# Two-block transformer on one core: the router's products with its weights stationary and both token tiles moving, its scores turned back by TensorE

## The chip, the cores and the metric

The kernel runs on one core of a Trainium2 chip. The metric is the time of one execution on the device in microseconds (us), the median of several runs. Engines are named as in the profile: PE is TensorE (PEld its loading of stationary operands), DVE VectorE, ACT ScalarE, POOL GpSimd, SP SyncE, which issues the loads.

## The reference

256 tokens of 1024 features pass a first block of two layers (gated feed-forward, a hybrid attention, gated feed-forward) and a second block of two layers. A layer of the second block is a mixer with a layer norm, and then this, on which the change works:

```python
ple = (p[i] @ ple_w_proj[i]) * jax.nn.sigmoid(x @ ple_w_gate[i])
ffn = grouped_moe(x, router_w, router_bias, moe_w1[i], moe_w3[i], moe_w2[i])
x = layer_norm_2(DEEPNORM_ALPHA * x + ffn + ple, ln_ffn_g[i], ln_ffn_b[i])

def grouped_moe(x, router_w, router_bias, w1, w3, w2):   # 16 experts in 4 groups, 2 chosen of one group
    scores = jax.nn.sigmoid((xt @ router_w).astype(F32))          # 256 x 16
    sel = scores + router_bias.astype(F32)
    grp_score = jnp.sum(lax.top_k(grp, TOP_K)[0], axis=-1)
    ...
    gates = jnp.sum(jax.nn.one_hot(idx, N_EXPERTS, dtype=F32) * w[..., None], axis=1)
    h = jax.nn.silu(jnp.einsum('td,edf->etf', xt, w1)) * jnp.einsum('td,edf->etf', xt, w3)
    h = h * gates.T[:, :, None].astype(h.dtype)
    y = jnp.einsum('etf,efd->td', h, w2)
```

## The kernel before

Tokens are two tiles of 128 (t = 0 and 1). The token rows `x` are turned by TensorE into `xt_hi` and `xt_lo`, a high part in a reduced format and the rest of it, each 128 x 8 x 256: features on the partitions, tokens along the row. Weights come in units of 1 MB on SyncE's queue into a ring of six buffers, and each is split the same way, the high part by ScalarE (line 1413), the low part by VectorE (line 1869). A product is three matmuls (`mm3`, lines 627 to 631; in the trace L629, L630, L631): high by high, high by low, low by high. `four` (line 649) does four blocks of 128 features, that is twelve matmuls, of one unit for one token tile: the tokens are stationary and 512 columns of weights move. `four` can call something ahead of its last block, `meanwhile`.

`before_experts` is written once for each engine and runs in both layers of the second block. On TensorE (line 1160) it does, in this order: `route(0)`, the router's product for tile 0, 24 matmuls with 128x128 tokens stationary and the router's 16 columns moving; `four` with the first unit for tile 0; the turn of tile 1 (`turn_x(1)`, eight transposes, which wait for VectorE's layer norm of that tile, line 1970); `four` with the second unit for tile 0; `route(1)`; `four` with both units for tile 1, each followed by a release of its unit (`unit_used`); one more unit for both tiles; a wait for `gates_ready`; five small products that number the chosen tokens (line 1188); the last unit; the turn of the small input `p`; the gather of the first experts' tokens (line 1154); the projection of `p`.

On ScalarE (line 1742) `scores(t)` takes the sigmoid of the 16 scores of a tile's 128 tokens (line 1745) into `r_s`, with splits of weights between the two. On VectorE (line 2415) come the low part of tile 1, two splits, and then the routing decisions: lines 2425 to 2462, some forty small operations one behind the other, up to `gates_ready`.

The experts (`gathered_experts`) run in eight pairs. Six buffers of 2 MB hold a pair's weights. `load_experts` (line 361) gives the order of the loads: the buffer of the first load is free when the stage begins, the next two wait for the first unit released in `before_experts`, two more for the third, one for the fourth, and the first two loads of the second pair for the end of the stage (`unit_used`); every later load waits until TensorE has used its buffer (`moe_used`). All of them stand in SyncE's one queue.

Of the kernel before, what the change touches and what calls it, by code (L numbers as in the profile page):

```python
# [19 lines left out]
ALU = mybir.AluOpType  # L20
# [6 lines left out]
P = 128  # L27
T = 256
TT = T // P
# [97 lines left out]
def program(nc, a, out):  # L127
    with ExitStack() as ctx:
# [6 lines left out]
        def sem(name):  # L135
            return ctx.enter_context(nc.semaphore(name))
# [133 lines left out]
        routed = sem("routed")  # L270
        route_sig = sem("route_sig")
# [121 lines left out]
        def carve(tensor, at, *dims):  # L393
            n = int(np.prod(dims))
            v = tensor[:, at:at + n]
            if len(dims) == 1:
                return v
            names = "abcd"[:len(dims)]
            return v.rearrange(f"p ({' '.join(names)}) -> p {' '.join(names)}",
                               **{k: d for k, d in zip(names[1:], dims[1:])})  # L400
# [72 lines left out]
        ple_gate = carve(work, 0, TT, D)  # L473
        r_s = carve(work, 13600, TT, N_EXPERTS)
# [160 lines left out]
        def _(pe):  # L635
# [524 lines left out]
            def before_experts(l):  # L1160
                def route(t):
                    pe.wait_ge(xt_lo_ready, seen(xt_lo_ready, 2))
                    for k in range(KD):
                        mm = mm3(pe, h_bank[t][:, 0:N_EXPERTS], xt_part(k, t), (rw_hi[:, k, :], rw_lo[:, k, :]),
                                 k == 0, k == KD - 1)
                    mm.then_inc(routed, 1)

                pe.wait_ge(rw_lo_ready, 1)
                route(0)
                w = []  # L1170
                for u in range(2):
                    w.append(unit(4))
                    four(y_bank[0][0][:, :], w[u], u, 0)
                    if u == 0:
                        turn_x(1)
                route(1)
                for u in range(2):
                    four(y_bank[1][0][:, :], w[u], u, 1).then_inc(unit_used, 1)
# [220 lines left out]
        def _(act):  # L1399
# [342 lines left out]
            def before_experts(l):  # L1742
                def scores(t):
                    act.wait_ge(routed, seen(routed))
                    act.activation(r_s[:, t], h_bank[t][:, 0:N_EXPERTS], ACT.Sigmoid).then_inc(route_sig, 1)

                scores(0)
                high_xt(1)
                split_to(4)
                scores(1)  # L1750
# [104 lines left out]
        def _(dve):  # L1855
# [559 lines left out]
            def before_experts(l):  # L2415
# [7 lines left out]
                dve.wait_ge(route_sig, seen(route_sig, TT))  # L2423
                bias = router_b.rearrange("p (o e) -> p o e", o=1).broadcast_to([P, TT, N_EXPERTS])
                link(dve.tensor_tensor(r_sel, r_s, bias, ALU.add))
# [303 lines left out]
```

## Time and profile before

| | us |
|---|---|
| median of 3 runs | 1782.88 (1781.55 to 1783.09) |
| profiled execution | 1785.93 |
| its span, first to last instruction | 1784.2 |
| TensorE busy | 1714.1 (96%) |
| VectorE busy | 925.7 (52%) |
| ScalarE busy | 630.7 (35%) |
| mean granted clock of TensorE | 0.986 |

Times of the trace are microseconds from the start of the span. A row of a timeline gives start, duration, engine, line, operation, what is written and read, the shape (stationary rows * columns, then partitions x moving columns) and how many instructions were merged; in brackets stand the idle time of the engine before it and what ended it. Matmuls are pipelined: the duration of one is longer than the distance of two starts, and the distance is the pace. The granted clock is 1.00 at 2.4 GHz and 0.50 at 1.2 GHz.

### The profile page before, as it was taken

The page shows a single profiled execution, that of the slowest core. Times are in us where ns is not written, and L with a number is a line of the kernel's source. Part 1 is how long each engine was busy: PE and PEld are TensorE (multiplying, and loading weights), DVE is VectorE, ACT ScalarE, POOL GpSimd, SP SyncE. Part 2 cuts the span into 40 slices and gives each one's busy share as a digit, 9 for nine tenths or more (in the row PEclk, how much of TensorE's full clock was granted, in tenths as well). Part 3 has the DMA queues.
Part 4 walks back from the last instruction along what each step waited for, and adds up shares of the span by engine and source line. Part 5 has one row for each costly group of instructions (what it writes and reads, how often), then busy time and mean ns, then how long its engine had stood idle before and what let it go on. Part 6 is the DMA issues. An engine that isn't in the chain of part 4 may idle for free.

```text
span 1784.2 us, 21897 instructions
## 1 busy us (share of the span) xinstructions
PE 1714.1 (96%) x8828; PEld 1244.3 (70%) x8828; DVE 925.7 (52%) x1342; ACT 630.7 (35%) x826; POOL 108.8 (6%) x89
## 2 busy tenths in 40 slices
PE   7999999999999999999899998999997999999996
PEld 6888777778878887777787787644443877744442
DVE  4754757674555546676685587511114566511113
ACT  4544443454425444443544364111112354111110
POOL 1000060000000000602000000000000000000000
PEclk9999999999999999999999999999998999999998
DMA  7555540655555555406454434899997533899994
GB/s 297 189 188 188 190 164 7 232 186 188 188 189 188 188 188 192 182 6 233 162 188 165 152 140 167 354 409 428 428 428 312 195 118 129 346 415 426 430 425 209
DMA packets 46803, 419.79 MB, mean 235 GB/s; under 512 B 5280, under 2 KB 5280, under 8 KB 8832
## 3 DMA queue, kind: packets, MB, share of 16 engines
q1 hardware_dynamic: 43200, 405.82, 58.2%
q0 software_dynamic: 3520, 12.78, 2.1%
q8 instruction: 62, 1.02, 0.2%
q14 instruction: 21, 0.17, 0.0%
HBM read 417.53 MB, written 1.05 MB: 235 GB/s over the span
## 4 chain that ended last, share of the span: by engine, by line
PE 83%; DVE 7%; DMA 4%; ACT 3%; POOL 1%; issue 1%; DVEq 0%; SPq 0%; POOLq 0%; ACTq 0%
PE hh L1237 11%; PE y L629 10%; PE y L631 10%; PE y L630 10%; PE hh L629 8%; PE hh L631 8%; PE hh L630 8%; DMA wide<-pairs 3%; PE turn L1154 3%; PE hh L1269 3%; PE turn L1269 3%; DVE w_lo L1869 2%; ACT w_hi L1413 1%; PE y L1281 1%; DMA raw<-units 1%; PE turn L747 1%
## 5 line engine op out<-in xcount | busy, mean ns | idle before, releaser
L1869 DVE TENSOR_TENSOR w_lo<-raw,w_hi 128x2048 fp32r<-128x2048 f32 x181 | 411.2, 2290 | 154.3 <-ACT w_hi L1413 153.5
L1413 ACT ACTIVATE w_hi<-raw 128x2048 fp32r<-128x2048 f32 x193 | 365.3, 1912 | 70.3 <-DMA raw<-units 66.1
L629 PE MATMUL hh<-w_hi,xt_hi 128*128 128x512 f32 x704 | 280.5, 398 | 8.0 <-DVE w_lo L1869 4.8
L631 PE MATMUL hh<-w_hi,xt_lo 128*128 128x512 f32 x704 | 276.0, 392 | 0.0
L630 PE MATMUL hh<-w_lo,xt_hi 128*128 128x512 f32 x704 | 275.5, 391 | 0.0
L1237 PE MATMUL hh<-wide,work 128*64 128x512 f32 x880 | 197.7, 599 | 4.8 <-DMA wide<-pairs 4.8
L629 PE MATMUL y<-w_hi,xt_hi 128*128 128x512 f32 (+1 forms) x464 | 184.8, 398 | 6.1 <-DVE xt_lo L2410 3.1
L630 PE MATMUL y<-w_lo,xt_hi 128*128 128x512 f32 (+1 forms) x464 | 180.5, 389 | 0.0
L631 PE MATMUL y<-w_hi,xt_lo 128*128 128x512 f32 (+1 forms) x464 | 180.4, 389 | 0.0
L629 PEld LDWEIGHTS hh<-w_hi,xt_hi 128*128 128x128 f32 x704 | 133.1, 189 | 36.6 <-DVE w_lo L1869 5.2
L631 PEld LDWEIGHTS hh<-w_hi,xt_lo 128*128 128x128 f32 x704 | 132.9, 189 | 28.6
L629 PE MATMUL y<-w_hi,ht_hi 128*128 128x512 f32 x368 | 145.7, 396 | 6.9 <-DVE w_lo L1869 6.7
L630 PEld LDWEIGHTS hh<-w_lo,xt_hi 128*128 128x128 f32 x704 | 133.3, 189 | 26.5
L1237 PEld LDWEIGHTS hh<-wide,work 128*64 128x64 f32 x880 | 61.9, 138 | 126.5 <-issue 117.4
L631 PE MATMUL y<-w_hi,ht_lo 128*128 128x512 f32 x368 | 144.2, 392 | 0.0
L630 PE MATMUL y<-w_lo,ht_hi 128*128 128x512 f32 x368 | 144.0, 391 | 0.0
L1431 ACT ACTIVATE gate_h<-hh 128x256 f32<-128x256 f32 x88 | 33.4, 383 | 214.0 <-PE hh L631 213.8
L629 PEld LDWEIGHTS y<-w_hi,xt_hi 128*128 128x128 f32 x464 | 89.0, 192 | 26.5 <-DVE xt_lo L1976 3.6
L569 POOL TENSOR_TENSOR rstd<-moments,minus_half 128x1 f32<-128x1 f32 x20 | 21.4, 1070 | 1345.1 <-DVE moments L1962 1345.1
L631 PEld LDWEIGHTS y<-w_hi,xt_lo 128*128 128x128 f32 x464 | 89.1, 192 | 18.1
L630 PEld LDWEIGHTS y<-w_lo,xt_hi 128*128 128x128 f32 x464 | 89.2, 192 | 16.3
L629 PEld LDWEIGHTS y<-w_hi,ht_hi 128*128 128x128 f32 x368 | 69.5, 189 | 24.2 <-DVE w_lo L1869 8.0
(344 smaller groups left out, 1957.8 us busy)
## 6 DMA issues: line engine op xcount, KB each, us to landing
raw<-units SPq DMA_DIRECT2D x193, 1024.0 KB
wide<-pairs SPq DMA_DIRECT2D x85, 2048.0 KB
late<-pairs SPq DMA_DIRECT2D x7, 1024.0 KB
raw<-pairs SPq DMA_DIRECT2D x7, 1024.0 KB
spare<-pairs SPq DMA_DIRECT2D x2, 2048.0 KB
xt_wide<-pairs SPq DMA_DIRECT2D x2, 2048.0 KB
ln_gb<-ln_g POOLq DMA_DIRECT2D x6, 512.0 KB, 3.9
ln_gb<-ln_b POOLq DMA_DIRECT2D x6, 512.0 KB, 5.5
```

What stands on the lines that cost most here:

```text
L569: pool.tensor_tensor(rstd[:, t], moments[:, t, 1:2], minus_half[:, 0:1], ALU.pow).then_inc(rstd_ready, 1)
L629: pe.matmul(dst, left[0], right[0], start=start, stop=False)
L630: pe.matmul(dst, left[0], right[1], start=False, stop=False)
L631: return pe.matmul(dst, left[1], right[0], start=False, stop=stop)
L747: mm = pe.transpose(turn_bank[0][:, k * T + t * P:k * T + (t + 1) * P], h[:, t, k * P:(k + 1) * P], ident[:, :])
L1154: mm = pe.matmul(dst[:, k * P:(k + 1) * P], x[:, t, at * P:(at + 1) * P], pick[:, p, t, :], start=t == 0, stop=t == TT - 1)
L1237: mm = pe.matmul(dst[half(b), :], xe[:, p, 4 * u + k, half(b)], w[b][:, k, :], start=u == 0 and k == 0, stop=u == 1 and k == 3)
L1269: mm = pe.matmul(dst[half(b), :], turned[:, k, half(b)], w[b][:, k, :], start=k == 0, stop=k == 3)
L1281: mm = pe.matmul(y_bank[t][c][:, :], spread[:, p, t * P:(t + 1) * P], part[:, c, :], start=first and part is ye_hi, stop=last and part is ...
L1413: act.activation(hi[r][:, :], raw[r][:, :], ACT.Copy).then_inc(hi_ready, 1)
L1431: act.activation(gate_act[:, t], h_bank[t][:, 0:HALF], ACT.Silu).then_inc(gate_ready, 1)
L1869: dve.tensor_tensor(lo[r][:, :], raw[r][:, :], hi[r][:, :].bitcast(F32), ALU.subtract)\
```

## The change

The router's weights become the stationary operand, 128 x 16, and the high or low part of both token tiles moves, 256 columns. So one set of 24 matmuls gives all scores, as 16 rows of 256 tokens, in `h_bank[0]`. It stands where `route(1)` stood; `route(0)` is gone. ScalarE takes one sigmoid of 16 x 256 into `score_t`, a new name for a part of `work`. TensorE turns it back with two transposes (`turn_scores`) into `h_bank[1]`, 128 tokens by 16 scores for each tile; it does so within the first `four` for tile 1, ahead of its last three matmuls, behind a wait for the sigmoid. VectorE waits for these transposes (`route_turned`) instead of the sigmoids, adds the bias from PSUM, and copies the scores to `r_s`.

```diff
--- before.py
+++ after.py
@@ -268,6 +268,7 @@
         rw_hi_ready = sem("rw_hi_ready")
         rw_lo_ready = sem("rw_lo_ready")
         routed = sem("routed")
+        route_turned = sem("route_turned")
         route_sig = sem("route_sig")
         gates_ready = sem("gates_ready")
         p_loaded = sem("p_loaded")
@@ -471,6 +472,7 @@
 
 
         ple_gate = carve(work, 0, TT, D)
+        score_t = work[0:N_EXPERTS, 13824:13824 + T]
         r_s = carve(work, 13600, TT, N_EXPERTS)
         r_sel = carve(work, 13632, TT, N_EXPERTS)
         r_two = carve(work, 13664, 8, TT * N_GROUPS)
@@ -1158,24 +1160,31 @@
                 mm.then_inc(gathered[l], 1)
 
             def before_experts(l):
-                def route(t):
-                    pe.wait_ge(xt_lo_ready, seen(xt_lo_ready, 2))
+                def route():
                     for k in range(KD):
-                        mm = mm3(pe, h_bank[t][:, 0:N_EXPERTS], xt_part(k, t), (rw_hi[:, k, :], rw_lo[:, k, :]),
-                                 k == 0, k == KD - 1)
+                        mm = mm3(pe, h_bank[0][0:N_EXPERTS, 0:T], (rw_hi[:, k, :], rw_lo[:, k, :]),
+                                 (xt_hi[:, k, :], xt_lo[:, k, :]), k == 0, k == KD - 1)
                     mm.then_inc(routed, 1)
 
-                pe.wait_ge(rw_lo_ready, 1)
-                route(0)
+                def turn_scores():
+                    pe.wait_ge(route_sig, l + 1)
+                    for t in range(TT):
+                        mm = pe.transpose(h_bank[1][:, t * N_EXPERTS:(t + 1) * N_EXPERTS], score_t[:, t * P:(t + 1) * P],
+                                          ident[0:N_EXPERTS, 0:N_EXPERTS])
+                    mm.then_inc(route_turned, 1)
+
                 w = []
+                pe.wait_ge(xt_lo_ready, seen(xt_lo_ready, 2))
                 for u in range(2):
                     w.append(unit(4))
                     four(y_bank[0][0][:, :], w[u], u, 0)
                     if u == 0:
                         turn_x(1)
-                route(1)
+                pe.wait_ge(rw_lo_ready, 1)
+                pe.wait_ge(xt_lo_ready, seen(xt_lo_ready, 2))
+                route()
                 for u in range(2):
-                    four(y_bank[1][0][:, :], w[u], u, 1).then_inc(unit_used, 1)
+                    four(y_bank[1][0][:, :], w[u], u, 1, meanwhile=turn_scores if u == 0 else None).then_inc(unit_used, 1)
                 last = unit(4)
                 for t in range(TT):
                     mm = four(y_bank[t][1][:, :], last, 0, t)
@@ -1740,14 +1749,10 @@
                 stage_done(S5_UNITS)
 
             def before_experts(l):
-                def scores(t):
-                    act.wait_ge(routed, seen(routed))
-                    act.activation(r_s[:, t], h_bank[t][:, 0:N_EXPERTS], ACT.Sigmoid).then_inc(route_sig, 1)
-
-                scores(0)
                 high_xt(1)
                 split_to(4)
-                scores(1)
+                act.wait_ge(routed, l + 1)
+                act.activation(score_t, h_bank[0][0:N_EXPERTS, 0:T], ACT.Sigmoid).then_inc(route_sig, 1)
                 split_to(PLE_UNITS)
                 for j in range(2):
                     wait_units(2 * j + 2)
@@ -2420,9 +2425,12 @@
                 dve.tensor_copy(tri.rearrange("p a c -> p (a c)"), tri_ones).then_inc(dve_link, 1)
                 dve.wait_ge(dve_link, seen(dve_link))
 
-                dve.wait_ge(route_sig, seen(route_sig, TT))
+                dve.wait_ge(route_turned, l + 1)
                 bias = router_b.rearrange("p (o e) -> p o e", o=1).broadcast_to([P, TT, N_EXPERTS])
-                link(dve.tensor_tensor(r_sel, r_s, bias, ALU.add))
+                turned_s = h_bank[1][:, 0:TT * N_EXPERTS].rearrange("p (t e) -> p t e", t=TT)
+                dve.tensor_tensor(r_sel, turned_s, bias, ALU.add).then_inc(dve_link, 1)
+                dve.tensor_copy(r_s, turned_s).then_inc(dve_link, 1)
+                dve.wait_ge(dve_link, seen(dve_link, 2))
                 four = r_sel.rearrange("p t (g e) -> p (t g) e", g=N_GROUPS)
                 for i, (u, v, op) in enumerate(((0, 1, ALU.max), (0, 1, ALU.min), (2, 3, ALU.max), (2, 3, ALU.min))):
                     dve.tensor_tensor(r_two[:, i], four[:, :, u], four[:, :, v], op).then_inc(dve_link, 1)
```

## Rows read from the trace of the kernel before

**Rows 1.** The page, part 4: the chain that ended last, by engine.

```profile
PE 83%; DVE 7%; DMA 4%; ACT 3%; POOL 1%; issue 1%; DVEq 0%; SPq 0%; POOLq 0%; ACTq 0%
```

**Rows 2.** Timeline of TensorE, layer 0 before the experts.

```profile
1105.47 0.17 PE L629 MATMUL hh<-rw_hi,xt_hi 128*128 128x16 f32 x1
...
1108.07 0.49 PE L629 MATMUL y<-w_hi,xt_hi 128*128 128x512 f32 x1
...
1111.73 0.48 PE L629 MATMUL y<-w_hi,xt_hi 128*128 128x512 f32 x1
...
1114.55 0.17 PE L629 MATMUL hh<-rw_hi,xt_hi 128*128 128x16 f32 x1
...
1117.93 0.61 PE L629 MATMUL y<-w_hi,xt_hi 128*128 128x512 f32 x1
...
1121.33 0.41 PE L631 MATMUL y<-w_hi,xt_lo 128*128 128x512 f32 x1
...
1129.79 0.62 PE L1188 MATMUL hh<-slot_mem 128*128 128x16 f32 x5
```

**Rows 3.** Timeline of VectorE, the same stage.

```profile
1108.90 1.41 DVE L1970 SCALAR_TENSOR_TENSOR x_rows<-x_rows,rstd,ln_gb 128x512 f32<-128x512 f32 x2
...
1118.13 0.19 DVE L2425 TENSOR_TENSOR work<-work,params 128x32 f32<-128x32 f32 x1
...
1128.91 0.23 DVE L2462 TENSOR_SCALAR gates<-work 128x16 f32<-128x16 f32 x1
```

**Rows 4.** Timeline, VectorE's norm and TensorE's turn of the first tile.

```profile
1100.75 1.42 DVE L1970 SCALAR_TENSOR_TENSOR x_rows<-x_rows,rstd,ln_gb 128x512 f32<-128x512 f32 x2 [0.54 <-POOL rstd L569]
...
1101.56 1.32 PE L661 MATMUL turn<-ident,x_rows 128*128 128x128 f32 x8 [1.83 <-DVE x_rows L1970]
...
1102.63 0.48 PE L629 MATMUL y<-w_hi,xt_hi 128*128 128x512 f32 x1
```

**Rows 5.** Timeline of TensorE, products with 256 moving columns.

```profile
1078.06 0.28 PE L630 MATMUL hh<-xt_lo,w_hi 128*128 128x256 f32 x1
...
1083.56 0.28 PE L631 MATMUL hh<-xt_hi,w_lo 128*128 128x256 f32 x1
```

**Rows 6.** The page, its part 5: busy, mean ns of one; idle before.

```profile
L1431 ACT ACTIVATE gate_h<-hh 128x256 f32<-128x256 f32 x88 | 33.4, 383 | 214.0 <-PE hh L631 213.8
```

**Rows 7.** Timeline, two transposes and who reads them.

```profile
1315.07 0.44 PE L1249 MATMUL turn<-ident,work 128*128 128x128 f32 x2
...
1315.54 0.42 DVE L2542 TENSOR_SCALAR slot_mem<-turn 128x256 fp32r<-128x256 f32 x1 [5.25 <-PE turn L1249]
```

**Rows 8.** Timeline of VectorE and TensorE, layer 1.

```profile
1511.78 1.42 DVE L1970 SCALAR_TENSOR_TENSOR x_rows<-x_rows,rstd,ln_gb 128x512 f32<-128x512 f32 x2
...
1521.02 0.19 DVE L2425 TENSOR_TENSOR work<-work,params 128x32 f32<-128x32 f32 x1
...
1532.66 0.62 PE L1188 MATMUL hh<-slot_mem 128*128 128x16 f32 x5
```

**Rows 9.** SyncE's issues; stretches: length, engines' busy, clock, DMA share, GB/s.

```profile
1121.77 0.83 SPq L359 DMA_DIRECT2D wide<-pairs  x2
...
1145.63 0.83 SPq L359 DMA_DIRECT2D wide<-pairs  x2
...
1118.00:1119.00 1.00, 1.00 (x4) 0.81 (x3) 0.90 (x9) 1.00 (x1) 0.00 (x0) 0.50 0.00 0
1178.00:1179.00 1.00, 1.00 (x8) 0.29 (x6) 0.00 (x0) 0.34 (x1) 0.00 (x0) 1.00 0.65 262
```

**Rows 10.** Timeline of TensorE behind two idle times, and stretches behind them.

```profile
997.83 0.50 PE L629 MATMUL hh<-w_hi,xt_hi 128*128 128x512 f32 x1 [2.12 <-ACT work L1665]
...
1751.70 1.77 PE L1237 MATMUL hh<-wide,work 128*64 128x512 f32 x6 [2.25 <-DMA wide<-pairs]
...
999.00:1000.00 1.00, 1.00 (x3) 0.78 (x3) 0.62 (x1) 0.00 (x0) 0.00 (x0) 0.50 0.00 0
1753.00:1754.00 1.00, 1.00 (x4) 0.24 (x2) 0.00 (x0) 0.00 (x0) 0.00 (x0) 0.50 1.04 442
```

## The prediction

> **What bounds the kernel now.** I read the page first. TensorE carries 83% of the chain that ended last [rows 1], so a stage is worth what it delays on TensorE, unless a wait takes over. The profiled execution took 1785.93 us, 1784.2 of it span; the median of the three runs is 1782.88. The sum below is made in times of the profiled execution, and its difference is put on the median.
>
> Then the timeline of TensorE in layer 0's stage before the experts [rows 2]. Products of the router run twice: 24 matmuls of 16 columns from 1105.47 to 1108.07 (2.60 us) and 24 more from 1114.55 on, 0.11 us each. Between and behind them stand groups of 12 matmuls of 512 columns; the group from 1111.73 to 1114.55 takes 2.82 us. From 1121.33 to 1129.79 there are 37 in 8.46 us, 0.229 us each. No row of TensorE from 1105.47 to 1129.79 carries idle time.
>
> The timeline of VectorE [rows 3] shows the second line of work: the second tile's rows are normalised by 1108.90 + 1.41 = 1110.31; the routing decisions start at 1118.13 and their last step ends at 1128.91 + 0.23 = 1129.14. That start carries no idle time, so it follows VectorE's own splits and not the scores; by their pace the products end near 1117.2. TensorE comes to the products that need the gates at 1129.79, only 0.65 us after they are ready. That slack is the number on which this case turns: the change takes work from TensorE, but its gates come by VectorE.
>
> Last the loads [rows 9]. No bytes move at 1118, since the next expert weights wait for a freed unit; they are issued at 1121.77. Those of the second pair are issued at 1145.63, when TensorE has finished this stage. At 1178 the DMA engines drop to 262 GB/s: they have caught up with what TensorE releases. After such a point their position depends on TensorE's releases and not on when the stream began. So what counts per layer is when TensorE gets into the experts.
>
> **Part by part, layer 0.** The first 24 small matmuls go, and the 12 wide ones behind them start 2.60 us earlier, at 1105.47, and end near 1108.3. Then TensorE turns the second tile, which VectorE finishes at 1110.31 as before: nothing in its path changed. For the first tile the same hand-over is in the trace: normalised at 1100.75 + 1.42 = 1102.17, next wide matmul at 1102.63 [rows 4], 0.46 us. So the next 12 start at 1110.77 and not 1111.73: of 2.60 us only 0.96 is left, the rest turns into a wait for VectorE of about 1.4 us. Behind the waiting transposes are queued all matmuls of TensorE; ScalarE and VectorE wait for the turned tile and get it 0.9 us earlier.
>
> They end at 1110.77 + 2.82 = 1113.59. The high and low halves of the turned tile, for which the router waits, are in time: before, TensorE came to the second small products as long after the transposes as now, and without idle time.
>
> The new router is 24 matmuls with 16 columns stationary and 256 moving. No row has this form. From below its pace is 0.11 us (the old form), from above 0.229 us (512 columns). I take the row with 256 moving columns and 128 stationary: 46 steps from 1078.06 to 1083.56 [rows 5], 0.12 us. That makes 2.88 us (bounds 2.6 and 5.5), ending at 1116.47.
>
> The Trainium skill, TensorE: Matmul & The Clock Gate, section LDWEIGHTS, has a load take time by its stationary columns, so that 16 would cost next to nothing. Its section Back-to-back issue gap gives 262 cycles for 256 moving columns, which at 2.4 GHz is an estimate of 0.109 us: 2.62 us for 24 where the row makes it 2.88, and the sum 0.26 us less per layer. The same page's section on Fast Weight Load speaks against the change: only loads of 128 columns that aren't FP32 are fast. No run here shows a load of 16 columns.
>
> Nine wide matmuls follow, 2.82 - 3 x 0.229 = 2.13 us, to 1118.60. They cover ScalarE's sigmoid. Its row has 128x256 at 383 ns [rows 6]; with a hand-over of 0.1 us it is done near 1117.0, and 1.6 us of cover is left. Were that gone, TensorE would wait on it with all its queue. Two transposes of 16 columns each follow. The nearest rows are two of 128 columns: start at 1315.07, VectorE reads them at 1315.54 and TensorE is busy on them for 0.44 us [rows 7]. So 0.47 us until VectorE and 0.44 of TensorE (bounds 0.2 and 0.8). VectorE starts on the decisions at 1119.07, not at 1118.13: it has ended its splits 0.9 us earlier than before and now waits for this turn. The added copy of the scores costs a step, 0.09 us. The decisions take 1129.14 - 1118.13 = 11.01 us as before, and the hand-over to TensorE 0.10 (half of the normalising ended at 1100.75 + 0.71 = 1101.46, the transposes started at 1101.56 [rows 4]). TensorE gets the gates at 1130.27, against 1129.79: 0.48 us later.
>
> TensorE itself is there at 1118.60 + 0.44 + 39 x 0.229 = 1127.97. It saved 1.82 us and then waits 2.30 us for VectorE. Behind that wait are its next 24 matmuls, the turn of the small input, the gather for the first experts, and SyncE's loads that these release.
>
> The same sum in layer 1 [rows 8]: rows normalised at 1511.78 + 1.42 = 1513.20; 0.46 + 2.82 + 2.88 + 2.13 + 0.47 later VectorE starts, at 1521.96 (before: 1521.02); 0.09 + 11.01 + 0.10 make 1533.16 against 1532.66, 0.50 us later. Both layers: 0.98 us later.
>
> Expert loads: the unit that releases them is used up near 1118.60 + 0.44 + 2 x 0.229 + 0.4 = 1119.9 instead of 1121.33 + 0.41 = 1121.74 [rows 2], so they start 1.8 us earlier. I cost that gain at nothing. Four slots and the extra one are all that may be loaded before TensorE has ended the stage, and the next wait for its releases (the load at 1145.63, then the drop at 1178) is 0.48 us later than before. Were these points not binding, the earlier start would be worth up to 1.8 us a layer.
>
> **The clock.** Before, the second small products are followed by half clock, 1.2 GHz: from 1117.93 to 1121.33 eight wide matmuls take 3.40 us [rows 2], where 8 x 0.229 is 1.83, so 1.57 us are lost; the granted clock is 0.50 at 1118 [rows 9]. Much of that was harmless, since TensorE had slack to the gates. The change takes these products away, and the 1127.97 is worked out without that loss. But it makes a new quiet stretch: 2.30 us between starts, some 2.1 as the trace counts idle time, with the five small products behind it (0.47 us). In the trace, idle times of 2.12 us (at 997.83) and 2.25 us (at 1751.70) were followed by half clock, with 0.50 granted at 999 and at 1753 [rows 10]. An idle time of 1.83 us was not: the matmul behind the transposes there lasts 0.48 us, where one at half clock lasts 0.61 [rows 4, 2]. Of this layer's two stretches of small products only the second was. So I give each layer's wait somewhat under an even chance of a half-clock stretch, which then lies on TensorE's path in full: 1.57 us. One of the two layers hit is the likeliest: 0.98 + 1.57 = 2.55 us, a span of 1786.75 for the profiled 1784.2 and 1785.4 on the median.
>
> **Rivals.**
> 1. No layer is hit: 0.98 us later, 1783.9. For it speaks that 1.83 us of idle time kept the full clock.
> 2. Slower side: both layers are hit, 0.98 + 2 x 1.57 = 4.12 us, 1787.0. It decides where both waits for the gates are followed by half clock; for it speaks that both rows above 2 us lost the clock, against it that the first stretch of small products, 2.60 us long, did.
> 3. Faster side: VectorE isn't late, because the gates' slack is larger than I think, and TensorE's whole saving of 1.82 us a layer arrives: 3.64 us less, 1779.2. The 0.65 us of slack speak against it.
> 4. The change doesn't make the products cheap: 16 stationary columns count for little, and the new products (2.88 us) are followed by half clock like the old ones, in front of the turned scores. Then the decisions start up to 1.57 us later in a layer: 0.98 + 1.57 per layer hit, 1785.4 or 1787.0. Its upper bound of pace, 0.229 us, would cost 2.6 us a layer and give 1789.1.
>
> **How the numbers follow.** One stretch hit 0.42, none 0.32, both 0.14, the products as in rival 4 0.07, the whole saving or most of it 0.05. The predicted time is that of the first, 1785.4. The range takes in rivals 1 and 2 with the bounds of the small costs (the page's pace and the lower bound for the transposes take 0.5 us a layer off, to 1782.9, and a fraction of a microsecond of slack gained to about 1782): 1781.9 to 1787.3. Faster or slower by over 0.2% (3.57 us, about what a measurement of this kernel can tell from no change) is below 1779.3 or above 1786.45. Faster has only the full case of rival 3: 0.04. Slower has rival 2 and a part of rival 4: 0.16. The rest is 0.80.
>
> **What would show it.** No 16-column router matmuls; 24 of 256 columns at 0.12 us. Idle time of TensorE of 1.3 to 1.5 us before the turn of the second tile. VectorE idle before its first routing step, until the two transposes. TensorE idle for 2.1 us before the five small products, where it had none. First expert load behind the spare one 1.8 us earlier, the one at 1145.63 later. Half clock behind the gates' wait or not decides between the forecast and rivals 1 and 2. I am wrong at the root if TensorE doesn't wait for the gates, or if the end of the experts moves with the first loads instead of with TensorE's entry.

## The result, and the profile after

| | before | after |
|---|---|---|
| median, 13 runs each, us | 1782.2 (1778.33 to 1784.76) | 1784.99 (1783.6 to 1787.33) |
| ratio after / before, 95% interval | | 1.0016 (1.0009 to 1.0024) |
| profiled execution, us | 1785.93 | 1783.6 |
| its span, us | 1784.2 | 1781.9 |

The change costs 2.8 us by the medians. That is less than the 0.2% that the prediction took as a change, but the interval of the ratio does not hold 1, so the changed kernel is slower, by little. The two profiled executions alone point the other way, 2.3 us faster. That is the first lesson of the case, and the section on the experiments comes back to it: the stages have to be compared one by one, and not the two spans.

The timeline of TensorE in layer 0 after the change (start, duration, engine, line, operation, operands, shape; in brackets idle time and what ended it), with ScalarE's sigmoid and VectorE's first step of the decisions and its last. Lines of the products are L631 to L633 here, of the turns L663, of the small products L1197.

```profile
1108.23 0.39 PE L633 MATMUL y<-w_hi,xt_lo 128*128 128x512 f32 x1
1109.93 1.32 PE L663 MATMUL turn<-ident,x_rows 128*128 128x128 f32 x8 [1.31 <-DVE x_rows L1975]
1111.00 0.48 PE L631 MATMUL y<-w_hi,xt_hi 128*128 128x512 f32 x1
...
1113.84 0.28 PE L631 MATMUL hh<-xt_hi,rw_hi 128*16 128x256 f32 x1
...
1116.62 0.39 PE L631 MATMUL y<-w_hi,xt_hi 128*128 128x512 f32 x1
1116.82 0.37 ACT L1755 ACTIVATE work<-hh 16x256 f32<-16x256 f32 x1 [3.13 <-PE hh L633]
...
1118.79 0.29 PE L1172 MATMUL hh<-ident,work 16*128 16x16 f32 x2
1119.01 0.50 PE L631 MATMUL y<-w_hi,xt_hi 128*128 128x512 f32 x1
1119.18 0.19 DVE L2431 TENSOR_TENSOR work<-hh,params 128x32 f32<-128x32 f32 x1 [1.98 <-PE hh L1172]
...
1130.06 0.23 DVE L2470 TENSOR_SCALAR gates<-work 128x16 f32<-128x16 f32 x1
1130.35 0.72 PE L1197 MATMUL hh<-slot_mem 128*128 128x16 f32 x5 [2.21 <-DVE gates L2470]
1130.93 0.48 PE L631 MATMUL y<-w_hi,xt_hi 128*128 128x512 f32 x1
```

Against [rows 2, 3] the reader is to see four things. The turn of the second tile now waits 1.31 us for VectorE, so that the removal of the first 24 small matmuls (2.60 us) gives back only a part. The new 24 take 1116.62 - 1113.84 = 2.78 us. VectorE, which had no idle time ahead of its decisions, now waits 1.98 us for the two transposes. And TensorE, which went into the five small products without idle time, waits 2.21 us for the gates.

In layer 1 the same rows stand, and what follows the wait is different:

```profile
1531.55 0.93 PE L1197 MATMUL hh<-slot_mem 128*128 128x16 f32 x5 [2.21 <-DVE gates L2470]
1532.33 0.78 PE L631 MATMUL y<-w_hi,xt_hi 128*128 128x512 f32 x1
1532.90 0.63 PE L632 MATMUL y<-w_lo,xt_hi 128*128 128x512 f32 x1
...
1535.03 0.54 PE L631 MATMUL y<-w_hi,xt_hi 128*128 128x512 f32 x1
1535.41 0.39 PE L632 MATMUL y<-w_lo,xt_hi 128*128 128x512 f32 x1
```

Matmuls of 512 columns last 0.63 us and not 0.39 until 1535. The stretches of that time say why (length, busy time of each engine, then the granted clock, the share of the DMA engines and GB/s): the clock is 0.50, that is 1.2 GHz.

```profile
1531.00:1532.00 1.00, 0.45 (x4) 0.46 (x4) 0.90 (x4) 0.00 (x0) 0.00 (x0) 0.96 1.07 459
1532.00:1533.00 1.00, 1.00 (x5) 0.90 (x5) 1.00 (x1) 0.00 (x0) 0.00 (x0) 0.50 1.03 426
1533.00:1534.00 1.00, 1.00 (x4) 0.81 (x3) 1.00 (x3) 0.00 (x0) 0.00 (x0) 0.50 0.92 393
```

SyncE's loads in layer 0, before in [rows 9] at 1121.77 and 1145.63, start 1.8 us earlier for the first group and 0.7 us later for the first of the second pair:

```profile
1120.00 9.00 SPq L360 DMA_DIRECT2D wide<-pairs  x4
...
1146.34 2.87 SPq L360 DMA_DIRECT2D wide<-pairs  x2
```

To set executions beside one another, all times below count from the end of the second tile's norm on VectorE, which the change doesn't touch (1109.12 + 1.42 = 1110.54 in layer 0 after; 1110.31 before by [rows 3]). "Entry" is the start of the first product of the experts on TensorE from there (L1246 after the change). After, it is 35.70 us in layer 0 and 37.27 in layer 1; the difference of the two is the half clock, 1.57 us. Before, it was 35.22 and 35.23. Each entry below is that of one execution, the profiled one, while the medians are those of all.

### The profile page after: what moved, and what is told of

Its sections match the earlier page's. It is cut to its first block, busy times and chain, and to the rows that moved or that the text cites. A ratio compares the mean times of both kernels' runs of the same rounds, so it can differ in the third digit from the quotient of the medians.

```text
span 1781.9 us, 21811 instructions
## 1 busy us (share of the span) xinstructions
PE 1706.8 (96%) x8784; PEld 1235.4 (69%) x8784; DVE 926.0 (52%) x1344; ACT 631.1 (35%) x824; POOL 108.8 (6%) x89
## 4 chain that ended last, share of the span: by engine, by line
PE 83%; DVE 9%; ACT 3%; DMA 3%; issue 1%; POOL 1%; DVEq 0%; SPq 0%; POOLq 0%; ACTq 0%
PE hh L1246 12%; PE y L631 10%; PE y L633 9%; PE y L632 9%; PE hh L631 8%; PE hh L633 8%; PE hh L632 8%; PE turn L1156 3%; PE hh L1278 3%; PE turn L1278 3%; DVE w_lo L1874 2%; PE y L1290 1%; DMA wide<-pairs 1%; ACT w_hi L1422 1%; DMA raw<-units 1%; PE turn L749 1%
## 5 line engine op out<-in xcount | busy, mean ns | idle before, releaser
L631 PE MATMUL hh<-w_hi,xt_hi 128*128 128x512 f32 x704 | 280.5, 398 | 8.2 <-DVE w_lo L1874 4.9
L633 PE MATMUL hh<-w_hi,xt_lo 128*128 128x512 f32 x704 | 276.1, 392 | 0.0
L1246 PE MATMUL hh<-wide,work 128*64 128x512 f32 x880 | 195.5, 594 | 2.2 <-DMA wide<-pairs 2.2
L631 PE MATMUL y<-w_hi,xt_hi 128*128 128x512 f32 (+1 forms) x464 | 183.6, 396 | 6.2 <-DVE xt_lo L2415 3.1
L633 PE MATMUL y<-w_hi,xt_lo 128*128 128x512 f32 (+1 forms) x464 | 179.4, 387 | 0.0
L631 PEld LDWEIGHTS hh<-w_hi,xt_hi 128*128 128x128 f32 x704 | 133.3, 189 | 36.8 <-DVE w_lo L1874 5.3
L633 PEld LDWEIGHTS hh<-w_hi,xt_lo 128*128 128x128 f32 x704 | 133.1, 189 | 28.6
L631 PE MATMUL y<-w_hi,ht_hi 128*128 128x512 f32 x368 | 146.2, 397 | 6.9 <-DVE w_lo L1874 6.7
L1246 PEld LDWEIGHTS hh<-wide,work 128*64 128x64 f32 x880 | 61.6, 137 | 122.0 <-issue 117.8
L633 PE MATMUL y<-w_hi,ht_lo 128*128 128x512 f32 x368 | 144.4, 392 | 0.0
L631 PEld LDWEIGHTS y<-w_hi,xt_hi 128*128 128x128 f32 x464 | 88.6, 191 | 26.5 <-DVE xt_lo L1981 3.6
L633 PEld LDWEIGHTS y<-w_hi,xt_lo 128*128 128x128 f32 x464 | 88.3, 190 | 17.8
L631 PEld LDWEIGHTS y<-w_hi,ht_hi 128*128 128x128 f32 x368 | 69.8, 190 | 24.2 <-DVE w_lo L1874 8.0
```

Of the source, the lines that this page charges most:

```text
L631: pe.matmul(dst, left[0], right[0], start=start, stop=False)
L633: return pe.matmul(dst, left[1], right[0], start=False, stop=stop)
L1246: mm = pe.matmul(dst[half(b), :], xe[:, p, 4 * u + k, half(b)], w[b][:, k, :], start=u == 0 and k == 0, stop=u == 1 and k == 3)
```

## The experiments

Theory A, the prediction's: the experts end with TensorE's entry; what the change costs is VectorE's lateness and, above all, half clock behind the new wait for the gates. Theory B: that half clock belongs to one execution, and the loss is somewhere else, in the load stream, which starts earlier, or in the form of the products. All kernels but old_form_moved, before2 and before3 are the changed kernel with the edit that is shown.

**The changed kernel again.** No edit.

> The changed kernel once more, as the reference for the other three. Theory A (VectorE's late gates and the half clock behind TensorE's wait for them): idle time of 2.2 us before the five small products in both layers, half clock behind it in about one layer of two, 2 to 3.5 us slower than the kernel before. Theory B (the difference lies elsewhere and the wait for the gates is harmless): the same idle time, but the stages from the second tile's norm to the end of the experts are no longer than in the kernel before.

Measured: 1785.70 us, ratio 1.0018 (1.0010 to 1.0027). Entry 37.26 and 37.31 us: half clock behind the wait in both layers. So what layer 0 gets is not fixed, though the wait is 2.2 us each time.

**Fill the wait.** Ten matmuls that nobody reads stand ahead of the wait for the gates:

```diff
+                for _ in range(10):
+                    pe.matmul(turn_bank[1][:, :], xt_hi[:, 0, 0:P], xt_hi[:, 2:4, :].rearrange("p k t -> p (k t)"),
+                              start=True, stop=True)
                 pe.wait_ge(gates_ready, seen(gates_ready))
```

> The changed kernel with ten extra matmuls of 512 columns, whose result nobody reads, in TensorE's wait for the gates. They take 10 x 0.229 = 2.29 us of a wait of 2.37 us from start to start, so the gates come no earlier and TensorE goes on at the same moment, but with a full array. Theory A: no half clock behind the wait in either layer, 1 to 2 us faster than the changed kernel, 0.5 to 1.5 us slower than the kernel before. Theory B, or the wait not being what lowers the clock: as the changed kernel within 0.5 us.

Measured: 1781.73 us, ratio 0.9994 (0.9985 to 1.0003), 4.0 us below the changed kernel in the same set of runs. Its timeline of TensorE:

```profile
1127.81 2.43 PE L1194 MATMUL turn<-xt_hi 128*128 128x512 f32 x10
1130.18 0.72 PE L1200 MATMUL hh<-slot_mem 128*128 128x16 f32 x5
1130.76 0.49 PE L631 MATMUL y<-w_hi,xt_hi 128*128 128x512 f32 x1
```

The small products start 19.82 us from the norm, as without the filling (19.81), so it delays nothing; the idle time is gone, the clock stays full in both layers, and the entry is 35.70 in both. Nothing else was altered. The direction is that of theory A, but the gain of 4.0 us is twice what was expected at most. The expectation had counted on about one layer hit, and both were; the entries of the two profiled executions make it 3.2 us. This shows that the loss of the changed kernel is the clock behind the wait, and not the wait as such, the form of the products or the loads.

**Turn the scores earlier.** `turn_scores` ahead of the second of the four blocks, behind three matmuls and not nine (`at` is 1 for it, 3 elsewhere):

```diff
-                    if meanwhile is not None and k == 3:
+                    if meanwhile is not None and k == at:
```

> The changed kernel with the two transposes of the scores behind three of the wide matmuls instead of nine, so 6 x 0.229 = 1.37 us earlier. ScalarE's sigmoid ends about 0.6 us behind the router's products, three wide matmuls take 0.7, so it is just covered. VectorE starts the decisions 1.37 us earlier, 18.44 us from the norm of the second tile to the five small products instead of 19.81 (before: 19.48), the wait shrinks to 0.8 us and no half clock follows. Theory A: 1.04 us a layer ahead of the kernel before, 2 us faster than it and 4 to 5 us faster than the changed kernel. Theory B (the loads set the end of the experts, and an earlier entry is worth nothing): level with the kernel before or less than 0.7 us faster.

Measured: 1779.52 us, ratio 0.9982 (0.9973 to 0.9991). TensorE and VectorE in layer 0:

```profile
1116.61 0.37 ACT L1755 ACTIVATE work<-hh 16x256 f32<-16x256 f32 x1 [3.13 <-PE hh L633]
...
1117.20 0.29 PE L1172 MATMUL hh<-ident,work 16*128 16x16 f32 x2
...
1117.60 0.19 DVE L2431 TENSOR_TENSOR work<-hh,params 128x32 f32<-128x32 f32 x1 [0.59 <-PE hh L1172]
...
1128.77 0.72 PE L1197 MATMUL hh<-slot_mem 128*128 128x16 f32 x5 [0.85 <-DVE gates L2470]
1129.35 0.48 PE L631 MATMUL y<-w_hi,xt_hi 128*128 128x512 f32 x1
```

It is 6.2 us faster than the changed kernel in the same set, where 4 to 5 were expected, and 2.3 faster than the kernel before, where 2 were. The decisions start 1.38 us earlier against the norm (7.27 and not 8.65), the wait shrinks to 0.85 us, no half clock follows in either layer, and the entry is 34.31 in both. Where the score transposes stand sets the length of the wait.

**One product per tile, the first in the wait for the second tile.** As turn_early, with 128 columns moving for each tile and `route(0)` ahead of `turn_x(1)`, where TensorE idles:

```diff
                     if u == 0:
+                        pe.wait_ge(rw_lo_ready, 1)
+                        route(0)
                         turn_x(1)
-                route()
+                route(1)
```

> The router's weights stay stationary, but each token tile moves by itself (128 columns): tile 0 ahead of the turn of the second tile, where TensorE waits 1.3 us, tile 1 where the change has its products; the transposes behind three matmuls. 24 matmuls of 128 columns should take 1.4 to 1.6 us. The first set fills the wait, the second takes 1.3 us less than the changed kernel's 2.8. Then VectorE's own splits (done 6.7 us behind the norm) start the decisions again. Theory A: 17.9 us from the norm to the small products, 1.6 us a layer ahead of the kernel before, 3 us faster than it. Theory B: less than 1 us faster. If 24 such matmuls take 2.6 us as the old ones did, it is like the earlier turn, 2 us faster.

Measured: 1779.63 us, ratio 0.9985 (0.9976 to 0.9994), 2.2 us below the kernel before, where theory A had 3. The pace of the new form, in the timeline of TensorE:

```profile
1108.46 0.22 PE L631 MATMUL hh<-xt_hi,rw_hi 128*16 128x128 f32 x1
1108.52 0.22 PE L632 MATMUL hh<-xt_lo,rw_hi 128*16 128x128 f32 x1
...
1128.46 0.72 PE L1199 MATMUL hh<-slot_mem 128*128 128x16 f32 x5 [1.58 <-DVE gates L2472]
```

24 of them take 0.06 us each, and the first 24 are free: the 1.3 us of idle time ahead of the turn are gone. VectorE no longer waits for the scores, so its own splits bind the start of the decisions (6.71 from the norm). A wait of 1.58 us stays, with full clock behind it in both layers. The entry is 33.72, 0.6 us a layer below turn_early, yet the time is the same within the intervals.

**The old form at the new place.** The kernel before with both sets of 16 moving columns where the new products stand, and both sigmoids behind ScalarE's second split:

```diff
-                pe.wait_ge(rw_lo_ready, 1)
-                route(0)
                 w = []
...
-                route(1)
+                pe.wait_ge(rw_lo_ready, 1)
+                pe.wait_ge(xt_lo_ready, seen(xt_lo_ready, 2))
+                for t in range(TT):
+                    route(t)
```

> The kernel before with one thing moved: both sets of 24 small products in their old form (tokens stationary, 16 columns moving) stand where the change has its one set, and both sigmoids behind them; nothing is turned back. From the norm of the second tile: wide products end at 3.3 us, 48 small ones at 3.3 + 5.3 = 8.6, decisions from 9.1 (before 7.8, changed kernel 8.65), gates 20.1. Theory A: 5.3 us of small products are followed by half clock in both layers, TensorE comes to the five small products at 8.6 + 48 x 0.229 + 1.6 = 21.2 instead of 19.5, so 1.7 us a layer and 3.4 us in all slower than before: the place costs, not only the form. Theory C (the form of the products is what matters, their place is not): about as before, since TensorE's work is the same.

Measured: 1787.80 us, ratio 1.0029 (1.0019 to 1.0039), 5.0 us slower where 3.4 were expected; entries 36.92 and 40.17. In layer 0 half clock stands behind the 48 small matmuls, for 3.4 us. In layer 1 it falls within them, at 1517.66, and lasts 10.2 us: the rest of the small ones go at 0.21 us each, and the decisions start 11.27 us from the norm, in layer 0 9.29. Layer 0, then a row of layer 1:

```profile
1118.57 0.36 PE L631 MATMUL hh<-rw_hi,xt_lo 128*128 128x16 f32 x1
1118.78 0.77 PE L629 MATMUL y<-w_hi,xt_hi 128*128 128x512 f32 x1
...
1518.03 0.36 PE L630 MATMUL hh<-rw_lo,xt_hi 128*128 128x16 f32 x1
```

At this place the new form is the cheaper one: by 2.9 us in the entries of both layers (77.09 against a mean of 74.16), by 1.1 to 2.2 in the medians, though the intervals overlap, and the 2.9 rest on one execution of the old form with a long stretch in it. It takes a second set away, and it keeps the clock up in front of the scores. The old form loses more in the same place, so it isn't by the form of its products that the change loses.

**A longer wait.** Five more steps on VectorE's chain, each of which adds zero, ahead of the gates:

```diff
+                for _ in range(5):
+                    link(dve.tensor_scalar(r_two[:, 7], r_two[:, 7], 0.0, None, ALU.add))
```

> The changed kernel with five extra small operations of VectorE (they add zero) in its decisions: 5 x 0.2 = 1.0 us more of waiting, 3.2 us of idle time. Theory A: half clock follows in both layers; 20.8 us from norm to small products and 38.3 to the experts, 2.0 us slower than the changed kernel where that is hit in both layers too. If the experts take up a late entry by themselves (the loads behind them have some slack), it is less than 1 us slower than the changed kernel.

Measured: 1789.73 us, ratio 1.0037 (1.0024 to 1.0050). The wait is 3.21 and 3.23 us and half clock follows in both layers; the entries are 38.28 and 39.73. In layer 1 the clock falls within the wait, at 1535.20, for 6.8 us, and the small products themselves are slow, 1.23 us and not 0.72:

```profile
1534.00:1535.00 1.00, 0.00 (x0) 0.00 (x0) 0.83 (x6) 0.00 (x0) 0.00 (x0) 1.00 0.99 410
1535.00:1536.00 1.00, 0.53 (x3) 0.53 (x3) 0.93 (x3) 0.00 (x0) 0.00 (x0) 0.60 1.10 459
1536.00:1537.00 1.00, 1.00 (x5) 1.00 (x5) 1.00 (x1) 0.00 (x0) 0.00 (x0) 0.50 0.96 410
```

One microsecond more on VectorE's chain in each layer made the entries 3.85 us later in sum (78.01 against 74.16): 2.0 us for itself, and nearly as much again in clock. Against the kernel before the median is 6.9 us up, where the changed kernel's was 2.8 and 3.9: 3 to 4 us for a wait that was expected to cost 2.0 where both layers are hit.

**Filled wait, loads later.** As fill, and the two loads behind the spare one wait for the second unit released and not the first:

```diff
-        for s, free in enumerate((q - 5, q - 4, q - 4, q - 2, q - 2, q - 1)):
+        for s, free in enumerate((q - 5, q - 3, q - 3, q - 2, q - 2, q - 1)):
```

> The kernel with the ten extra matmuls in the wait, and SyncE's first expert loads behind the spare one tied to the second freed unit instead of the first, so 12 matmuls or 2.7 us later (12.2 us behind the norm; before 11.5, now 9.5). If the start of the load stream counted, 47 loads would end 2.7 us a layer later and the kernel would be 5 us slower than the filled one. If the entry of TensorE sets the stream, as the prediction had it, the 47 loads end within 0.5 us of where they did (245.5 us behind the norm) and the time is within 1 us of the filled one.

Measured: 1782.54 us, ratio 0.9996 (0.9987 to 1.0004). SyncE starts them 12.19 us from the norm, where fill does at 9.47:

```profile
1124.33 6.26 SPq L360 DMA_DIRECT2D wide<-pairs  x4
...
1147.90 0.82 SPq L360 DMA_DIRECT2D wide<-pairs  x2
```

2.7 us of lead in these loads are worth nothing that can be measured (0.2 us in the distances to the kernel before), with the entries as they were (35.67 and 35.61). The changed kernel shows how the lead is lost: in its stretches, the DMA engines move 402 GB/s up to 1146 and then wait for TensorE's releases, 225 GB/s, where before the change they moved 426 in the same four microseconds.

```profile
1120.00:1146.00 26.00, 23.79 (x125) 19.92 (x123) 15.37 (x56) 5.14 (x8) 0.00 (x0) 1.00 0.97 402
1146.00:1150.00 4.00, 4.00 (x20) 1.35 (x20) 2.13 (x6) 0.00 (x0) 0.00 (x0) 1.00 0.71 225
```

**The best of it.** As per_tile, with VectorE's copy of `tri` ahead of its splits (it stood at the head of the decisions) and the turn of the small input ahead of the wait for the gates:

```diff
+                turn_h(p=True)
                 pe.wait_ge(gates_ready, seen(gates_ready))
...
+                link(dve.tensor_copy(tri.rearrange("p a c -> p (a c)"), tri_ones))
                 low_xt(1)
                 split_to(4)
```

> The per-tile form with VectorE's copy of the triangular matrix ahead of its wait for the turned tile (0.3 us less in front of the decisions) and TensorE's turn of the small input in the wait for the gates (0.44 us of work off the path behind it). Entry into the experts at 33.7 - 0.3 - 0.4 = 33.0 us behind the norm instead of 33.7. Theory A with no slack: 1.5 us faster than the per-tile form. If by now the load stream sets the end of the experts, as the equal times of the two faster kernels suggest: level with it, within 0.7 us, and the 47 loads end no earlier than 243.5 us behind the norm.

Measured: 1778.21 us, ratio 0.9973 (0.9962 to 0.9984): faster than both kernels, 4.6 us below the kernel before in the same set of runs. The decisions start 6.39 us from the norm, the wait is 0.78 and 0.80 us, the clock stays full, the entries are 33.37 and 33.40.

**How often the clock falls.** The changed kernel and the kernel before, two more executions each, without an edit.

> The changed kernel a third time, one look, to count in how many layers half clock follows the wait of the five small products for the gates. So far it did in 3 of 4 layers (35.70 us from the end of the second tile's norm to the first expert product without it, 37.26 to 37.31 with it). Theory of the wait: idle time of 2.2 us in both layers, and 37.3 us in at least one of them. Rival, that the stretch belongs to one execution and not to the wait: 35.7 in both.

> The changed kernel a fourth time, one look, with the same purpose as the third. Theory of the wait: 2.2 us of idle time ahead of the five small products in both layers, and in at least one of them half clock behind it, with 37.3 us from the end of the second tile's norm to the first expert product. Rival, no tie to the wait: 35.7 us in both layers.

> The kernel before a second time, one look. It has no wait at the five small products, and its half clock stood behind the second tile's set of small products in both layers (1117.94 and 1520.71 us). Theory: the same place in both layers, and about 35.2 us from the end of the second tile's norm to the first expert product. Rival, half clock falls anywhere: another place, or none.

> The kernel before a third time, one look, with the same purpose as the second. Theory: half clock behind the second tile's set of small products in both layers, none behind the five small products, and 35.2 us from the end of the second tile's norm to the first expert product. Rival: half clock in another place or missing.

Measured (one execution each, 1785.95, 1785.59, 1781.01 and 1783.82 us): the changed kernel has half clock behind the wait in all four layers, entries 37.30, 37.31, 37.27 and 37.21. With the first two executions that is 7 layers of 8. An example is layer 0 of again2, where the clock falls 1.6 us after the small products have started, at 1131.64:

```profile
1131.38 0.40 PE L631 MATMUL y<-w_hi,xt_hi 128*128 128x512 f32 x1
1131.62 0.59 PE L632 MATMUL y<-w_lo,xt_hi 128*128 128x512 f32 x1
1132.01 0.63 PE L633 MATMUL y<-w_hi,xt_lo 128*128 128x512 f32 x1
```

The kernel before missed its expectation, and there is more to learn from it. In its layer 0 half clock stands behind the first set of small products in both executions, where it had stood behind the second alone (in before2 it stands behind both). TensorE's timeline of before2:

```profile
1108.06 0.26 PE L631 MATMUL hh<-rw_hi,xt_lo 128*128 128x16 f32 x1
1108.17 0.67 PE L629 MATMUL y<-w_hi,xt_hi 128*128 128x512 f32 x1
1108.63 0.63 PE L630 MATMUL y<-w_lo,xt_hi 128*128 128x512 f32 x1
...
1112.59 1.03 PE L661 MATMUL turn<-ident,x_rows 128*128 128x128 f32 x8
```

The turn of the second tile starts at 1112.59 here, though VectorE had ended its norm at 1110.41: the decisions start 9.37 us from the norm and not 7.82, in before3 too. And in layer 1 of before2 no set is followed by half clock (in before3 the second is, as expected); TensorE then comes to the gates early and waits:

```profile
1530.61 0.72 PE L1188 MATMUL hh<-slot_mem 128*128 128x16 f32 x5 [0.85 <-DVE gates L2462]
```

The entries of the kernel before are 36.74 and 34.76 us in before2, and 36.33 and 35.25 in before3. The mean of its three profiled executions is 71.18 us for both layers, and not the 70.45 of the one on which the prediction was made.

**How long must a wait be?** The prediction let the clock fall behind idle times of 2.12 and 2.25 us and not behind 1.83, by one row for each. The same waits stand in all 14 traces, and these bear out no such limit. Counted is half clock that begins within 2 us of the end of the wait. The wait of 1.83 us for the norm of the first tile, in layer 0 [rows 4], was followed by half clock in four of 14: in after, best, old_form_moved and longer_wait. The wait of 2.1 us near 998 [rows 10] was so in 14 of 14, one of 3.1 us near 1090 in nine of 14, and it kept the clock in those same four and in fill. One of 1.65 us near 758, with transposes and narrow products behind it, lost it in eight of 14, the kernel before on which the prediction was made among them. Layer 0 after the change:

```profile
1100.20 1.32 PE L663 MATMUL turn<-ident,x_rows 128*128 128x128 f32 x8 [1.83 <-DVE x_rows L1975]
...
1102.64 0.63 PE L632 MATMUL y<-w_lo,xt_hi 128*128 128x512 f32 x1
```

So the length of a wait alone does not say whether the clock falls; what else does is left open.

**All of it in one table.** Entry of both layers in sum, its distance to the 71.18 us of the kernel before, and the measured distance of the median to that of the kernel before in the same set of runs:

| kernel | idle before the small products | half clock behind it | entries, sum | to 71.18 | measured |
|---|---|---|---|---|---|
| changed, mean of 4 executions | 2.2 | 7 of 8 | 74.16 | +2.98 | +2.79, again +3.91 |
| fill | 0 | 0 of 2 | 71.40 | +0.22 | -0.06 |
| fill_late | 0 | 0 of 2 | 71.28 | +0.10 | -0.25 |
| turn_early | 0.85 | 0 of 2 | 68.62 | -2.56 | -2.27 |
| per_tile | 1.6 | 0 of 2 | 67.43 | -3.75 | -2.16 |
| best | 0.8 | 0 of 2 | 66.77 | -4.41 | -4.58 |
| longer_wait | 3.2 | 2 of 2 | 78.01 | +6.83 | +6.94 |
| old_form_moved | 0 | (at the 48 products, 2 of 2) | 77.09 | +5.91 | +5.01 |

The time moves with TensorE's entry into the experts, nearly one to one, from -4.6 to +6.9 us; every distance of the entries lies within the interval of its ratio. The base of 71.18 is itself the mean of 70.45, 71.50 and 71.58. per_tile's median is the farthest off. The transfers hint at a reason: counted from the first load behind the spare one, the bytes of 47 expert loads (2 MB each) have moved 244.1 and 244.3 us from the norm in turn_early, and 243.5 and 244.4 in per_tile, so that its 0.6 us earlier entry doesn't show there in layer 1. But best enters 0.3 us earlier still, has 243.5 and 244.0, and its median is 1.4 us lower than per_tile's. Whether the load stream begins to bind there is left open.

The two spans can be told apart by the same marks. The two entries made the profiled execution after the change 2.5 us later (0.48 and 2.04), and the norm in layer 0 0.2 us. Two other stretches, which the change doesn't touch, took it back. From the entry in layer 1 to the end of the experts' last product it needs 218.8 us, before it needed 221.7: there TensorE waited for a load at 1751.70 and had half clock behind it [rows 10]; in neither of the other two executions of the kernel before does a row stand there that costs as much (218.8 and 219.3 us). And from the entry in layer 0 to the norm in layer 1 it needs 365.5 us, before it needed 367.7. The other two of the kernel before need 364.6 and 366.9 there, so this stretch moves by 3 us between executions of one kernel; why was not looked into. 2.5 + 0.2 - 2.9 - 2.2 are the 2.3 us of the spans, and their sign comes from stretches that vary, not from the change.

## Why the prediction was right

The forecast was 1785.4 us, 2.55 above the kernel before; measured were 1784.99 and 2.79. Step by step, with layer 0 of the profiled execution:

- **The wait for the second tile** came as worked out: 1.31 us of idle time (1.35 in layer 1), forecast about 1.4. From norm to the next wide matmul 1111.00 - 1110.54 = 0.46, as [rows 4] had it.
- **The new products** were forecast at 2.88 us, with 2.6 and 5.5 as bounds: 2.78 measured, 0.116 us each.
- **The turn of the scores**: 1119.18 - 1118.79 = 0.39 us to VectorE, forecast 0.47. TensorE lost 0.22 us to it (1118.79 to 1119.01) and 0.1 ahead of it, forecast 0.44. With the pace, this is why the decisions start 8.65 us from the norm and not 8.76, against 7.82 before.
- **VectorE late for TensorE**: the small products start 0.33 and 0.35 us later than before, forecast 0.48 and 0.50. In the kernels where the clock stays full the entry is nevertheless 0.48 us later than in [rows 2] (35.70 and 35.22), since the five products last 0.72 us where they wait for the gates (in fill too, which has no idle time) and 0.62 where the gates are there. The sum was right by two small errors.
- **The wait for the gates**: 2.21 us in both layers, forecast about 2.1.
- **The clock**: 1.57 us a stretch, as forecast from [rows 2]. But the chance was mis-sized. I had given each layer somewhat under an even chance, and one layer of two as the likeliest; the runs show 7 layers of 8, so that two layers of two is the common case. The profiled execution, with one, was the rarer one. The evidence for the chance was thin: I read "1.83 us keeps the clock" from one row, and that row kept it in ten traces of 14; an idle time of 1.65 us at 757.68 in the trace of the kernel before, with 0.50 granted from 759.54 on, did not enter into it.
- **The base**: I took the entry of the kernel before from one execution, where half clock stood behind the second set in both layers and cost little. Its mean over three executions is 0.73 us later for both layers, since half clock also falls behind the first set, in front of the turn, where it lies on the path.

These last two nearly cancel: 1.75 stretches and not 1 add 1.2 us, the later base takes 0.7 off; 0.96 + 1.75 x 1.57 - 0.73 = 2.98, the table's number. So the mechanism was right, and that the median was met within half a microsecond is in part luck: the base and the frequency were both too low. From one profiled execution the frequency could not have been known; that the kernel before has stretches of its own that move about could have been: [rows 2] show two equal sets of small products in each layer, of which one was hit.

The rivals: none hit (1783.9) was refuted by all four executions. Both hit (1787.0) is what most executions have, though the median is lower, as the base is. The whole saving (1779.2) fell with the 2.21 us of wait. That half clock would follow the new products fell: from 1116 to 1118 the granted clock is 1.00 in the profiled execution, and in none of the others does a stretch begin there. That the earlier loads bring nothing was borne out by fill_late.

In rows, 2.2 us of idle time with five products of 16 columns behind it lost the clock in 7 layers of 8, and 0.8 to 1.6 us in none of eight (turn_early, per_tile, best, layer 1 of before2 and layer 0 of before3). That holds for this place; elsewhere in the traces 1.65 and 1.83 us lost it at times. The Trainium skill, TensorE: Matmul & The Clock Gate, section HAM oscillation, tells of a kernel whose short bursts of matmuls are parted by waits for transfers and which starts each burst at the lower clock. The traces here agree in that half clock follows a wait, here one for VectorE. They differ in that it didn't stand at the start of the burst: the clock fell 0.4 to 1.6 us after the small products had started.

## What to carry to other kernels

A saving on the engine that looks like the bound is worth only the slack of what it waits for next: here 0.65 us of slack stood against 1.8 us saved, and the rest became idle time that cost more than was saved, because the clock fell behind it. When work is taken from TensorE, give the engine that feeds it the same head start (here, the two transposes six matmuls earlier: from 1.0016 to 0.9982), or put useful work in the hole. And take the base of a comparison from several executions, at a mark that the change doesn't touch, before believing a difference of a few microseconds.

## What the runs showed of the hardware

- The pace of matmuls with 16 stationary columns went with their moving columns: 0.116 us with 256, 0.060 us with 128. With 128 stationary and only 16 moving columns it is 0.11 us [rows 2], so there something other than the moving columns sets it. Turning the product round so that the narrow operand is stationary, 24 matmuls serve a tile of 128 tokens in 1.44 us and not 2.60. The Trainium skill, TensorE: Matmul & The Clock Gate, section Back-to-back issue gap, gives some 81 ns for 128 moving columns in a sustained stream and 134 cycles alone, an estimate of 56 ns at 2.4 GHz; the row is near the second.
- Whether half clock followed the small products went with their form and not their length: 2.60 us of 16 moving columns were followed by it in five of six layers of the kernel before, behind one set or the other (in one layer behind both, so six of twelve sets), while 2.78 us of 256 moving columns were in none of 16 layers.
- In this stage a stretch at half clock lasted 3.4 us, but 6.8 in layer 1 of longer_wait and 10.2 in layer 1 of old_form_moved. One of 3.4 us made the entry 1.57 us later.
- One wait, two outcomes: idle times of 2.20 to 2.22 us in the same place kept the clock once and lost it seven times. When it was lost, the fall came from 0.4 us (layer 1 of the profiled execution) to 1.6 us after the small products had started. Elsewhere in the same 14 traces waits of 1.65, 1.83, 2.1 and 3.1 us lost it in eight, four, fourteen and nine, so a longer one isn't always the worse one.
